# A two-block transformer kernel: query units copied out of PSUM, a compressed-attention chain moved, and three weight units walked at two norms

## The reference

```python
# odd layer; h = rms_norm(x, norm_w[1])
proj = h @ w_in + b_in
fp, iv, qp, z = split(proj, 4)                    # 8 units of 128 columns each
logf = log(lb + (1 - lb) * sigmoid(fp))           # k = (1 - lb) * sigmoid(-fp)
q = silu(qp)                                      # the query units
o = hgrn2_chunkwise(heads(q), heads(k), heads(iv), heads(logf))
x = x + (rms_norm(o, head_norm) * silu(z)) @ w_out
# even layer, compressed branch
p_c = masked_softmax(q_blk @ k_cmp.T, cmp_end <= t)
out = gate * (p_c @ v_cmp) + ...                  # then * silu(z)
# ffn2
x = x + 0.5 * (silu(n @ w_gate) * (n @ w_up)) @ w_down    # n = rms_norm(x, ffn2_norm)
```

## Time and profile before

| what | value |
|---|---|
| median of 3 runs | 1013.21 us (1012.15 to 1013.81) |
| the profiled execution | 1012.79 us, of it 1011.0 us span |
| PE busy | 962.2 us, 95% |
| POOL busy | 646.2 us, 64% |
| ACT busy | 538.4 us, 53% |
| DVE busy | 464.3 us, 46% |
| chain that ended last | PE 57%, issue 22%, POOL 15%, DVE 3% |

### The profile page before, as it was taken

The page is one execution under the profiler, slowest core; times in us unless marked ns, Lnnn a source line. Parts: engine busy times, 40 slices in busy tenths (PEclk is TensorE's granted clock), DMA queues, the critical chain, the costliest instruction groups (busy, mean ns, idle before and its releaser), DMA issues.

```text
span 1011.0 us, 23200 instructions
## 1 busy us (share of the span) xinstructions
PE 962.2 (95%) x9036; PEld 923.5 (91%) x9036; DVE 464.3 (46%) x878; ACT 538.4 (53%) x791; POOL 646.2 (64%) x276
## 2 busy tenths in 40 slices
PE   5998999999899989999999999999999999999997
PEld 4988788899899979999999989999998999999996
DVE  5256424785754574433330133563584743334112
ACT  6577654675645676544444347665421654454441
POOL 2885333367699717877777747544313479878882
PEclk9999999999899999999999999999999999999999
DMA  8644213245433306555555544332002246555551
GB/s 336 209 153 143 85 64 104 71 140 165 154 120 104 126 22 188 167 176 178 173 181 167 177 137 146 126 125 85 3 3 87 91 149 206 184 185 185 187 179 51
DMA packets 39041, 139.79 MB, mean 138 GB/s; under 512 B 4272, under 2 KB 5552, under 8 KB 38832
## 3 DMA queue, kind: packets, MB, share of 16 engines
q1 hardware_dynamic: 38960, 138.62, 42.3%
HBM read 137.55 MB, written 1.05 MB: 137 GB/s over the span
## 4 chain that ended last, share of the span: by engine, by line
PE 57%; issue 22%; POOL 15%; DVE 3%; ACT 1%; DMA 0%; POOLq 0%; SPq 0%; DVEq 0%; ACTq 0%
PE ps L707 57%; POOL wlo L641 14%; DVE hT L1997 1%; DVE ivt L1970 1%; POOL rN L682 0%; DMA xT<-in_x 0%; ACT whi L1531 0%; DVE mixT L1961 0%; ACT rstd L1454 0%; DVE fxL L1961 0%; DVE aL L2007 0%; DVE hA L2358 0%; PE ps L1262 0%; DVE aL L1970 0%; POOLq L650 0%
## 5 line engine op out<-in xcount | busy, mean ns | idle before, releaser
L641 POOL TENSOR_TENSOR wlo<-ring,whi 128x1024 fp32r<-128x1024 f32 x251 | 602.3, 2418 | 321.5 <-ACT whi L1531 303.3
L1531 ACT ACTIVATE whi<-ring 128x1024 fp32r<-128x1024 f32 x253 | 266.7, 1060 | 170.0 <-PE ps L707 146.1
L707 PE MATMUL ps<-aH,whi 128*128 128x272 f32 (+1 forms) x1048 | 307.2, 293 | 13.6 <-issue 4.8
L707 PE MATMUL ps<-aH,wlo 128*128 128x272 f32 (+1 forms) x1048 | 301.1, 287 | 0.0
L707 PE MATMUL ps<-aL,whi 128*128 128x272 f32 (+1 forms) x1048 | 300.5, 287 | 0.0
L707 PEld LDWEIGHTS ps<-aH,whi 128*128 128x128 f32 x1048 | 200.0, 191 | 19.1 <-issue 9.2
L707 PEld LDWEIGHTS ps<-aL,whi 128*128 128x128 f32 x1048 | 200.0, 191 | 0.6 <-issue 0.5
L707 PEld LDWEIGHTS ps<-aH,wlo 128*128 128x128 f32 x1048 | 200.0, 191 | 0.0
L707 PE MATMUL ps<-fxH,whi 128*128 128x256 f32 x480 | 136.1, 284 | 4.2 <-POOL wlo L641 2.4
L707 PE MATMUL ps<-fxH,wlo 128*128 128x256 f32 x480 | 135.7, 283 | 0.0
L707 PE MATMUL ps<-fxL,whi 128*128 128x256 f32 x480 | 135.7, 283 | 0.0
(11 more groups left out here) (371 smaller groups left out, 1413.9 us busy)
## 6 DMA issues: line engine op xcount, KB each, us to landing
ring<-in_stream SPq DMA_DIRECT2D x253, 512.0 KB, 4.0
cst<-in_cst SPq DMA_DIRECT2D x1, 1325.0 KB, 12.5
xT<-in_x SPq DMA_DIRECT2D x4, 272.0 KB, 3.8
out<-hT SPq DMA_DIRECT2D x4, 256.0 KB, 2.4
row<-in_row SPq DMA_DIRECT2D x1, 898.0 KB, 9.2
cst<-in_cst SPq DMA_DIRECT2D x1, 640.0 KB, 10.0
mat<-in_mat SPq DMA_DIRECT2D x1, 576.0 KB, 13.4
vec<-in_vec SPq DMA_DIRECT2D x1, 135.0 KB, 4.0
```

Of the source, the lines that this page charges most:

```text
L641: nc.gpsimd.tensor_tensor(wlo[:, s, :], ring[:, s, :], whi[:, s, :].bitcast(F32), ALU.subtract).then_inc(S("w_split"), 1)
L707: return nc.tensor.matmul(out, lhsT, rhs, start=start, stop=stop, skip_group_check=True)
L1531: nc.scalar.activation(whi[:, v % SLOTS, :], ring[:, v % SLOTS, :], ACT.Copy).then_inc(S("w_high"), 1)
```

## The change

There are four edits.

1. Three units instead of two are walked at `norm1` (the HGRN layer's first units) and at the norm of `ffn2`. The new function `feature_trio` walks six tiles of the first two units, then six tiles of the third, then the last two tiles of the first two, then those of the third. `norm` follows it, and after that comes one unit fewer than before.
2. The query units 0 to 4 (before: 0 and 1) leave PSUM with DVE's first operation, the scaling by `rstd`. ACT adds the bias, in an instruction of its own ahead of the tanh. DVE's bias operation is gone for all eight. DVE's order between the prefix sums is new.
3. In the even layer DVE does the compressed softmax (`compressed`) ahead of the convolution of unit 18 and ahead of the product `gated`, which stood at unit 16.
4. At the last level before the eighth, DVE copies two of the four banks, makes the product, and copies the other two.

```diff
-            return fZ[:, 1 + m, :] if m < 2 else ps[...]
+            return fZ[:, 1 + m, :] if m < 5 else ps[...]
...
+            def feature_trio(u, g, t0, ready, tag, early):
+                xh, xl = acts(tag)
+                parts = [weights(u + j) + [bank(g + j)] for j in range(3)]
...
+                for k in range(early):
+                    for part in parts[0:2]:
+                        tile(k, *part)
+                for k in range(early):
+                    tile(k, *parts[2])
+                for k in range(early, KT):
+                    for part in parts[0:2]:
+                        m = tile(k, *part)
+                        if k == KT - 1:
+                            m.then_inc(S("w_used"), 1)
+                for k in range(early, KT):
+                    m = tile(k, *parts[2])
+                m.then_inc(S("w_used"), 1)
...
-                feature_pair(U_H, G_H, TM, ready)
+                feature_trio(U_H, G_H, TM, ready, "norm1", 6)
                 norm("norm1", T)
-                for j in range(2, H_UNITS - 1):
+                for j in range(3, H_UNITS - 1):
...
+                if tag == "ffn2":
+                    feature_trio(u0, g0, c0, ("norm_h", NORMS.index(tag) * KT), tag, 6)
+                else:
+                    feature_pair(u0, g0, c0, ("norm_h", NORMS.index(tag) * KT), tag)
                 norm(tag, TT - c0)
+                gate_up(0, 1, (1,) if tag == "ffn2" else (0, 1))
...
             def gate_tanh(m):
-                act.wait_ge(S("q_biased"), m + 1)
+                act.wait_ge(S("q_scaled"), m + 1)
+                func(query(m), query(m), ACT.Identity, bias=V("qp_b", m))
                 func(fQ[:, m, :], query(m), ACT.Tanh, "q_th", scale=0.5)
...
+                    if j == 18:
+                        convolved(j)
+                        gated()
...
+                scaled_query(0)
+                scanned(0)
+                subtracted(0)
+                scaled_query(1)
+                scanned(1)
+                scaled_query(2)
+                subtracted(1)
+                scaled_query(3)
+                gated_query(0)
+                for m in range(4, 8):
+                    gated_query(m - 3)
+                    scaled_query(m)
+                for m in range(5, 8):
+                    gated_query(m)
...
+                            banks_of(7, (0, 1))
+                            products(8)
+                            banks_of(7, (2, 3))
```

More of the change, by code:

```diff
@@ L1087, in ffn, with gate_up @@
                 xh, xl = acts(tag)
-                def gate_up(it, f4):
-                    for j in range(2 * f4, 2 * f4 + 2):
+                def gate_up(it, f4, only=(0, 1)):
+                    for j in [2 * f4 + i for i in only]:
                         pe.wait_ge(S("w_split"), it * 8 + (u0 + j + 1))
@@ L1102, in ffn @@
                     pe.wait_ge(S("meta_lo"), KT)
-                feature_pair(u0, g0, c0, ("norm_h", NORMS.index(tag) * KT), tag)
+                if tag == "ffn2":
+                    feature_trio(u0, g0, c0, ("norm_h", NORMS.index(tag) * KT), tag, 6)
+                else:
+                    feature_pair(u0, g0, c0, ("norm_h", NORMS.index(tag) * KT), tag)
                 norm(tag, TT - c0)
-                for f4 in range(1, 4):
+                gate_up(0, 1, (1,) if tag == "ffn2" else (0, 1))
+                for f4 in range(2, 4):
                     gate_up(0, f4)
@@ L2056, in even_in @@
                 between = {4: (small_columns,), 5: (forget,), 6: (gate_columns,), 8: (gate_maxima, compress), 10: (normalized, hidden),
-                           11: (rotated,), 14: (kc_n,), 15: (kc_rot,), 16: (gated,), 18: (compressed,)}
+                           11: (rotated,), 14: (kc_n,), 15: (kc_rot,), 18: (compressed,)}
                 for j in range(E_UNITS):
@@ L2063, in even_in @@
                         drain_pair(G_E + j, [vtok[:, :, (m + i) * P:(m + i + 1) * P] for i in range(2)], ROW["v"] + m * P)
-                    if E_QK <= j < E_QK + 8:
+                    if E_QK <= j < E_QK + 8 and j != 18:
                         convolved(j)
@@ L2305, in hgrn_in @@
                     if j in LEVEL_AT and LEVEL_AT[j] < 8:
[L2306 to L2307 removed]
+                        if LEVEL_AT[j] < 7:
+                            banks_of(LEVEL_AT[j], range(4))
+                            products(LEVEL_AT[j] + 1)
+                        else:
+                            banks_of(7, (0, 1))
+                            products(8)
+                            banks_of(7, (2, 3))
                     if gate and j < H_UNITS - 2:
@@ L2324, in values, with scaled_query, gated_query, scanned @@
                             "drained_v" if tt_ else "dve_step")
-            def sums_of_logarithms(i):
-                gates, keys = [ps[:, 4 + 2 * n:6 + 2 * n, :].rearrange("p a b -> p (a b)") for n in range(2)]
-                sums = fC[:, i * 4 * T:(i + 1) * 4 * T]
+            def scaled_query(m):
+                now = ps[:, (G_H + H_Q + m) % MM_BANKS, 0:T]
+                dve.wait_ge(S("w_used"), used_by(G_H + H_Q + m))
+                tt(query(m), now, rstd[:, 0:T], ALU.mult, "q_scaled")
+                if m < 5:
+                    dve.sem_inc(S("drained_v"), 1)
+                    dve_n["drained_v"] = dve_n["drained_v"] + 1
+            def gated_query(m):
+                dve.wait_ge(S("q_th"), m + 1)
+                stt(fQ[:, m, :], fQ[:, m, :], 1.0, query(m), ALU.add, ALU.mult, "q_gated" if m < 5 else "drained_v")
+            def scanned(i):
+                gates = ps[:, 4:6, :].rearrange("p a b -> p (a b)")
                 dve.wait_ge(S("f_log"), i + 1)
-                step(nc.vector.tensor_tensor_scan(sums, dif[:, 0, 0:4 * T], gates, 0.0, ALU.mult, ALU.add), "f_scan")
+                step(nc.vector.tensor_tensor_scan(fC[:, i * 4 * T:(i + 1) * 4 * T], dif[:, 0, 0:4 * T], gates, 0.0,
+                                                  ALU.mult, ALU.add), "f_scan")
+            def subtracted(i):
+                keys = ps[:, 6:8, :].rearrange("p b n -> p (b n)").rearrange("p (a b) -> p a b", a=4)
                 dve.wait_ge(S("k_log"), i + 1)
-                tt(fLK[:, 4 * i:4 * i + 4, :], keys.rearrange("p (a b) -> p a b", a=4), sums.rearrange("p (a b) -> p a b", a=4),
+                tt(fLK[:, 4 * i:4 * i + 4, :], keys, fC[:, i * 4 * T:(i + 1) * 4 * T].rearrange("p (a b) -> p a b", a=4),
                    ALU.subtract, "key_log")
@@ L2343, in twice_gated, with banks_of @@
                 stt(out, out, 1.0, ps[:, g % MM_BANKS, 0:T], ALU.add, ALU.mult, "drained_v")
-            def banks_of(lev):
-                for j in range(4):
+            def banks_of(lev, banks):
+                for j in banks:
                     dve.wait_ge(S("lev_s"), 4 * lev + j + 1)
```

5 lines of the change are left out of this document (4 added, 1 removed).

## The result

| what | before | changed |
|---|---|---|
| median (4 runs each) | 1013.51 us | 1029.59 us (1027.63 to 1032.22) |
| ratio | | 1.0156, 95% interval 1.0137 to 1.0174 |
| profiled execution | 1012.79, span 1011.0 | 1030.43, span 1028.6 |
| mean granted clock of the profiled one | 0.993 | 0.984 |

The change makes the kernel 16 us slower. The forecast was 1025.6 us, range 1018.5 to 1030.5. The measured time lies inside the range, but it is nearer to the price of the second rival (1029.8 us, the query edit gives nothing) than to the forecast, so the traces have to tell the two apart.

What follows compares the result with a forecast made beforehand. PE, busy for 95% of the span, was taken as the bound, so only its waits and clock count. The terms 6.7 + 5.1 + 6.2 - 4.2 - 1.3 + 0.3 = +12.8 us on 1012.79 gave 1025.6 us, range 1018.5 to 1030.5.

Steps and rivals of the forecast that it cites:

- the second rival: Query units: the query edit gives nothing, POOL's halves and level sums bind from unit 16 on; 1029.8 us, chance 0.12.
- edit 3, even layer: Compressed chain: the wait moves to the transposes and PE is slightly later; +0.3 us, bounds -1.6 and +1.0.
- walk at norm1, joint wait and 24 matmuls: At norm1 the walk starts 3.9 us later, awaiting unit 2's low half; sums after 72 matmuls, unit 4 +6.7 us.
- clock in that walk: Half clock behind each 5.9 us wait, at norm1 and ffn2: +2.3 us each, bounds 0 and 3.4.
- clock behind unit 4: Half clock after the wait before unit 4: 0 at norm1, +1.6 us at ffn2, bounds 0 and 2.8.
- edit 2, unit 4 to the pair 17 and 18: Query units: unit 14's 4.84 us wait goes, shorter POOL waits come at 16 and 17; -4.2 us, bounds -7.6 and 0.
- edit 4, level 8: Last level: the product awaits two bank copies instead of four, so level 8 starts earlier; -1.3 us, bounds -1.9 and 0.
- walk at ffn2: At ffn2's norm, later walk start and sums after 72 matmuls put unit 4 at 830.1 against 825.00: +5.1 us.
- The two waits ahead of each norm's unit 4: PE, with one unit fewer to fill the time, waits some 3.7 us at norm1 and 3.4 us at ffn2.
- the two of 5.95 us: PE's waits before the three-unit walks at norm1 and ffn2, released by unit 2's low half: some 5.9 us each.
- The third rival: Walks start as before, each unit waiting for its own halves only: 1013.3 us, or 1009.9 us; chance 0.10.

Runs made afterwards that it cites:

- edit 2 alone: The kernel before with the query units copied out of PSUM and nothing else of the change: 1012.3 us, 0.9992 of before.
- edits 2 and 4 together: The changed kernel with walks of two units and the compressed chain back at its old place: 1009.98 us, 0.996 of before.

## Why the prediction was right, and where its terms were off

The places of the prediction, as the lateness of the changed kernel's trace grows:

| step | predicted | measured in the traces |
|---|---|---|
| edit 3, even layer | +0.3 | +1.8 |
| walk at norm1, joint wait and 24 matmuls | +6.7 | +6.8 |
| clock in that walk | +2.3 | +2.8 |
| clock behind unit 4 | 0 | 0 |
| edit 2, unit 4 to the pair 17 and 18 | -4.2 | -3.5 |
| edit 4, level 8 | -1.3 | -1.2 |
| mixer, not touched | 0 | +1.5 |
| walk at ffn2 | +5.1 | +5.3 |
| clock in that walk | +2.3 | +2.5 |
| clock behind unit 4 | +1.6 | +1.5 |
| sum | +12.8 | +17.5 of 17.6 |

How they are read: the sums of squares moved from 228.33 to 239.71, 11.4 us. Of these, 1.8 came with the layer ahead (the wait began at 228.38 - 5.95 = 222.43, before at 222.64 - 1.99 = 220.65) and 72 matmuls took 11.33 us instead of 8.53, 2.8 more; 6.8 are left. From unit 4 (+11.3) to the pair (289.44 against 281.56, +7.9) the kernel gained 3.5. At level 8 it is +6.8, at level 0 it was +8.0. At ffn2 the sums moved by 16.2, of which 8.4 stood already at 643.18 and 2.5 are clock; 5.3 are left. The end of the span moved by 17.6, 1.5 more than unit 4.

**Right.** The mechanism of edit 1, to 0.2 us at either norm, because the function's first statement decides it and both engines' times were in the rows. The two waits ahead of each norm's unit 4 (3.46 and 3.24, foretold 3.7 and 3.4; the rows' own 0.67 + 2.84 would have made 3.5) and the two of 5.95 us (5.9). That the clock falls, and by how much: 6.8 us at the four places against 6.2. That norm1's second half clock is paid out of the waits at units 16 and 17, which shrank to 0.82 and 1.75 us from 1.93 and 1.82 in the kernel with two-unit walks, 1.2 us in all. PE had lost as much behind unit 4: at 250.12 us before it is 12.5 us late, at unit 4 it was 11.3. The third rival, each unit waiting only for its own halves, was built: even that costs 1018.01 - 1010.99 = 7.0 us, where twice 2.84 had been said, since the long waits ahead of unit 4 and the clock behind them stay.

The second rival is out by the trace: from unit 4 to the pair the kernel gained 3.5 us. Its reason was not empty, for the two waits that are left there are both for POOL's low halves. That the measured time stands near its price is chance: 1.5 us more than forecast came from edit 3, 1.5 from the mixer, 0.7 from edit 2 and 0.6 from the clock at the norms.

**Luck.** The time came out inside the range although some 3 us of it had no term: the half clock in the even layer and in the mixer. The range was wide enough, but no term of the sum stood for them.

**Mis-sized.** Edit 3 was to cost 0.3 us, bounds -1.6 and +1.0, and measured +1.8 in this trace and 0.1 to 3.1 in the runs. The wait moved as described: 2.46 us gone, 1.62 come (1.5 foretold), and the transposes were 0.4 us late. The rest came with the half clock behind them. What I left out was that a short wait can have a price by its place: behind 1.62 us among the small matmuls of the compressed branch six of seven traces have half clock, and neither of the two with the wait filled. I had given the clock terms only to waits that were new and long.

The query edit missed 0.7 us of its 4.2, by ACT: the bias instruction on a unit in SBUF takes 0.51 us and not the 0.43 of a tanh, so the eight take 4.0 us (277.03 to 281.01) instead of 3.4, and the high half of unit 16 comes later. ACT's rows, the fourth such pair and that half:

```profile
280.01 0.51 ACT L1481 ACTIVATE mixT<-mixT,vec 128x256 f32<-128x256 f32 x1
280.56 0.42 ACT L1481 ACTIVATE fQ<-mixT 128x256 f32<-128x256 f32 x1
281.01 1.06 ACT L1558 ACTIVATE whi<-ring 128x1024 fp32r<-128x1024 f32 x1
```

**Not foreseen.** Half clock in the mixer, which no edit touches. The Trainium skill, page "TensorE: Matmul & The Clock Gate", section "HAM oscillation — how this bites in real kernels", puts the loss on idle time between bursts. The walks and the filled waits agree: 11.04 us for the walk at ffn2 against 8.56 with the wait filled. The stretches at 90 and 623 us do not show it that way, since PE's busy time in front of them is 3.00 of 3 us at 88 and 2.61 of 3 us at 620 in the changed kernel. What stands in front of the first are 29 matmuls of 15 columns and others about as small; whether they are the reason, no run tells.

**Open.** Why the same rows from 87 us on are followed by half clock in some executions and not in others. Without edit 3 two of five traces have it, with edit 3 eight of nine, and PE's instructions up to there are the same. The half clock in the mixer stands in seven of the fourteen traces: in all five with a walk of three units and in both with unit 4's high half made early, and in none of the seven others. The one thing these seven share is a changed norm1, some 390 us ahead of the mixer; why that should matter, nothing here shows. And how much of edit 2 is left in the times: 3.5 us gained in one trace, between 2.6 gained and 0.9 lost in the runs of edit 2 alone, and 1.9 to 6.2 gained by edits 2 and 4 together.

## What to carry to other kernels

When a loop is widened to share a wait, look which statement asks for all its inputs at once: here one line that collected three pairs of weights cost 10 to 12 of some 18 us. Price a wait by its length and by the clock behind it, and a moved wait as a new one; a few cheap products in it can pay for themselves, if they are no longer than the wait (six matmuls in 1.62 us, 22 in 5.95 us here; 24 in 1.62 us gained nothing). Before taking credit from one trace, compare its mean clock with that of the other runs.

## What the runs showed of the hardware

- The time of a run of the kernel before goes with its mean granted clock: 1010.72 us at 0.995 and 1017.78 us at 0.988, in one series of 33. It is no rule without exception: the kernel with 12 products in the wait ran in 1013.73 and in 1017.67 us, both at 0.994.
- A float32 product written as one matmul of 256 columns ran as two, 0.225 us each (24 in 5.40 us), where those of the walk, on rounded halves, start 0.118 us apart.
- A wait of 2.0 us ahead of the walk at norm1 was followed by full clock in the kernel with two-unit walks and by half clock for 3.4 us (from 223.5) in the one with the early high half.
